# Cached attention of a four-layer decoder step: the last four value blocks of each layer are loaded into other buffers

## What is computed

```python
def memory_cross_attn(x, mem_k, mem_v, w_q, w_o):
    bsz, L, _ = x.shape
    q = (x @ w_q).reshape(bsz, L, X_HEADS, X_HEAD_DIM)
    s = jnp.einsum('blhd,bmhd->bhlm', q, mem_k.astype(q.dtype)).astype(F32) * (X_HEAD_DIM ** -0.5)
    p = jax.nn.softmax(s, axis=-1).astype(x.dtype)
    o = jnp.einsum('bhlm,bmhd->blhd', p, mem_v.astype(x.dtype)).reshape(bsz, L, D_MODEL)
    return o @ w_o
```

## Time and profile before

| what | value |
|---|---|
| median of three runs | 2028.56 us (2024.79 to 2032.39) |
| the profiled execution | 2023.7 us |
| its span, first to last instruction | 2021.8 us |
| TensorE busy (matmul) | 1951.7 us, 97% |
| VectorE, ScalarE, GpSimd busy | 62%, 46%, 50% |
| mean granted TensorE clock | 0.986 |
| HBM read and written | 292.16 MB and 29.61 MB, 159 GB/s over the span |

### The profile page before, as it was taken

One profiled execution on the slowest core, in us unless ns is written; L12 is line 12 of the kernel. 1 busy time (PEld: TensorE's weight loads), 2 busy tenths in 40 slices (PEclk: granted clock), 3 DMA queues, 4 the chain that ended last, 5 costly groups with the idle time before them and its releaser, 6 DMA issues.

```text
span 2021.8 us, 35611 instructions
## 1 busy us (share of the span) xinstructions
PE 1951.7 (97%) x13890; PEld 1760.9 (87%) x13890; DVE 1247.0 (62%) x2220; ACT 930.9 (46%) x1557; POOL 1010.1 (50%) x1249
## 2 busy tenths in 40 slices
PE   7999999998999999999999999999999999999997
PEld 5998989698888888897889999999997889999966
DVE  5988342426887778655137778777464158874452
ACT  3676522334655555342354444443242347773333
POOL 3776704036555565250346566666641347775602
PEclk8999999999999999999999999999999999999998
DMA  4444476635434444486353444444586344455860
GB/s 128 149 145 135 136 249 232 206 105 173 130 110 144 139 137 144 126 297 209 132 181 107 130 131 129 130 143 145 174 305 215 135 139 139 140 159 179 279 210 27
DMA packets 332615, 324.64 MB, mean 161 GB/s; under 512 B 19768, under 2 KB 313056, under 8 KB 332448
## 3 DMA queue, kind: packets, MB, share of 16 engines
q1 hardware_dynamic: 330944, 321.49, 49.8%
q10 hardware_dynamic: 1504, 0.87, 0.2%
HBM read 292.16 MB, written 29.61 MB: 159 GB/s over the span
## 4 chain that ended last, share of the span: by engine, by line
PE 56%; DVE 11%; ACT 4%; DMA 3%; issue 2%; POOL 1%; SPq 0%; DVEq 0%; ACTq 0%
PE ps L764 8%; PE ps L765 7%; PE ps L769 7%; PE ps L1449 4%; PE ps L1252 3%; PE ps L1458 2%; PE ps L1515 2%; PE ps L754 2%; PE ps L755 2%; PE ps L756 2%; DVE work L2534 2%; ACT wh L1704 1%; PE ps L1532 1%; PE ps L1562 1%; DMA cache_area<-cache_mem_v 1%
## 5 line engine op out<-in xcount | busy, mean ns | idle before, releaser
L1684 POOL TENSOR_TENSOR wl<-raw,wh 128x256 fp32r<-128x256 f32 x1216 | 1004.6, 862 | 983.9 <-ACT wh L1704 983.8
L1704 ACT ACTIVATE wh<-raw 128x1024 fp32r<-128x1024 f32 x304 | 311.8, 1053 | 205.2 <-PE ps L769 52.4
L764 PE MATMUL ps<-Hh,wh 128*128 128x320 f32 x1200 | 369.6, 322 | 2.6 <-DVE gate_area L2554 0.9
L765 PE MATMUL ps<-Hl,wh 128*128 128x320 f32 x1200 | 357.3, 311 | 0.0
L764 PEld LDWEIGHTS ps<-Hh,wh 128*128 128x128 f32 x1200 | 228.0, 190 | 10.4 <-DVE work L2418 1.8
L765 PEld LDWEIGHTS ps<-Hl,wh 128*128 128x128 f32 x1200 | 228.2, 190 | 2.2
L2249 DVE TENSOR_SCALAR work<-ps 128x512 f32<-128x512 f32 (+8 forms) x220 | 100.3, 474 | 171.0 <-PE ps L862 39.8
L769 PE MATMUL ps<-Hh,wl 128*128 128x320 f32 x1200 | 200.4, 309 | 0.0
L769 PEld LDWEIGHTS ps<-Hh,wl 128*128 128x128 f32 x1200 | 182.3, 188 | 0.1
L764 PE MATMUL ps<-Oh,wh 128*128 128x320 f32 x512 | 153.4, 312 | 3.7 <-DVE Ol L2995 3.7
L765 PE MATMUL ps<-Ol,wh 128*128 128x320 f32 x512 | 152.2, 310 | 0.0
(11 more groups left out here) (439 smaller groups left out, 3925.2 us busy)
## 6 DMA issues: line engine op xcount, KB each, us to landing
raw<-rg_w_in SPq DMA_DIRECT2D x128, 256.0 KB, 3.6
raw<-hg_w_in SPq DMA_DIRECT2D x128, 256.0 KB, 4.8
raw<-ssd_w_in SPq DMA_DIRECT2D x96, 256.0 KB, 4.0
work<-cache_mem_k SPq DMA_DIRECT2D x40, 512.0 KB, 6.2
raw<-rg_w_out SPq DMA_DIRECT2D x64, 256.0 KB, 3.5
raw<-x_w_k SPq DMA_DIRECT2D x64, 256.0 KB, 3.6
raw<-x_w_v SPq DMA_DIRECT2D x64, 256.0 KB, 3.8
raw<-x_w_q SPq DMA_DIRECT2D x64, 256.0 KB, 5.7
```

Of the source, the lines that this page charges most:

```text
L764: pe.matmul(ps[:, bank, 0:n], high(half, k), mh[:, k, 0:n], start=(k == 0), stop=False)
L765: pe.matmul(ps[:, bank, 0:n], high(half, k), ml[:, k, 0:n], start=False, stop=False)
L1684: ins = pool.tensor_tensor(out, src, wh[:, parted(n) % HALVES, r:r + 2].bitcast(F32), ALU.subtract)
L1704: act.activation(wh[:, nx.n % HALVES], raw[:, slot, :, half * P:(half + 1) * P], ACT.Copy).then_inc(hi_ready, 1)
```

## The change

Blocks 0 to 27 keep their buffers. Block 28 gets columns 5120 to 6143 of `work` (the prompt's memory keys), blocks 29 and 30 get the two halves of the turned keys, and block 31 gets buffer 4, in which value block 16 was. Block 28 is issued behind block 15 and ahead of block 16. Each of the three new buffers has a semaphore of its own for what has landed.

```diff
+        at_kb += [work[:, 5120:6144], work[:, 0:D], work[:, D:2 * D]]
+        KB_SLOT = [n % CACHED for n in range(28)] + [CACHED, CACHED + 1, CACHED + 2, 28 % CACHED]
 
         def cached_count(L, n):
 
-            return 16 * (L * len(range(n % CACHED, 32, CACHED)) + n // CACHED + 1)
+            return 16 * (L * KB_SLOT.count(KB_SLOT[n]) + KB_SLOT[:n + 1].count(KB_SLOT[n]))
...
-                    if n >= CACHED:
-                        sp.wait_ge(*past("at_kb_used", 32 * layer + n - CACHED + 1))
-                    sp.dma_start(at_kb[n % CACHED], src).then_inc(S(f"at_kb_in{n % CACHED}"), 16)
+                    slot = KB_SLOT[n]
+                    if slot in KB_SLOT[:n]:
+                        last = max(m for m in range(n) if KB_SLOT[m] == slot)
+                        sp.wait_ge(*past("at_kb_used", 32 * layer + last + 1))
+                    elif slot == CACHED:
+                        for h in range(2):
+                            sp.wait_ge(*past(f"at_k_out{h}", 32 * (layer + 1)))
+                    elif slot > CACHED:
+                        sp.wait_ge(*past("at_cs_full", 16 * (layer + 1)))
+                    sp.dma_start(at_kb[slot], src).then_inc(S(f"at_kb_in{slot}"), 16)
...
-                for n in range(CACHED, 32):
+                for n in [*range(CACHED, 16), 28, *range(16, 28), 29, 30, 31]:
                     cache(n)
...
                 def cached(n):
-                    pe.wait_ge(*past(f"at_kb_in{n % CACHED}", cached_count(L, n)))
-                    return at_kb[n % CACHED]
+                    pe.wait_ge(*past(f"at_kb_in{KB_SLOT[n]}", cached_count(L, n)))
+                    return at_kb[KB_SLOT[n]]
```

## The result

The changed kernel takes 2018.06 us (median of seven runs, 2010.39 to 2021.32) against 2028.56 us (seven runs, 2024.79 to 2032.39): ratio 0.9938, 95% interval 0.9923 to 0.9953. By that ratio it is 12.6 us less (9.5 to 15.6). The ratio is not the quotient of the two medians, which differ by 10.5 us only. Two later comparisons gave 0.9932 and 0.9937. The forecast was 2020.0 us in a range of 2013 to 2027. The kernel is faster by a little over 0.5%, to which I had given 0.25.

The account below looks back on a forecast made before the run. TensorE was taken to bound the kernel; 7.0 us of stall plus 1.5 us of clock, 8.5 us, took the profiled 2023.7 us to 2015.2. Adding 0.42% for the timed median gave 2020.0 us, range 2013 to 2027.

Parts of the forecast that it names:

- Stall of 29 to 31, 7.0 us: In four layers' attention, TensorE's waits for loads of value blocks 29 to 31 go away: 7.0 us in sum.
- Block 28 costs nothing: In SyncE's queue, loading block 28 early into the memory's keys costs nothing and by itself saves nothing.
- Blocks 29 and 30 go out behind the last scores: In layer 1, these loads issue at about 954.1 and 954.5 after the last score matmuls, needed 14 us after landing.
- Block 31 lands in time in first place: Issued at about 969.1 in layer 1, first in the queue, not fourth; lands 1.3 us early, without a wait.
- The tail behind block 31 moves along unchanged: From the last value block to the output projection, the same steps follow and hide nothing of the gain.
- TensorE's clock, 1.5 us: At the start of layer 3's output projection, the half-speed clock returns to full: 1.5 us, bounds 0 and 1.53.
- The sum: Over the whole kernel, 7.0 us of stall plus 1.5 us of clock give a gain of 8.5 us.
- Rival A: In the attention, block 31 stays late or part of the gain is given back: gain 3 to 5 us; chance 0.12.
- C: SyncE's queue hangs at block 28 waiting for the memory keys' stores: 2038 us or more; chance 0.02.
- D: Nothing changes, since the DMA engines can't bring the blocks earlier; chance 0.02.
- B: Half-clock stretches move elsewhere: two fewer give 2017 us, two more 2023; chances 0.12 and 0.10 for two or more.

Follow-up runs that it names:

- e7_28_in_place: The changed kernel with block 28 issued behind block 27, its old place, not behind block 15; ratio to the kernel before 0.9928.
- n1_same: The kernel before, run again with no edit; ratio to itself 0.9995, profiled span 2016.8 us.
- e4_gap: The changed kernel with TensorE made to wait for ScalarE copies ahead of value blocks 29 to 31 in all layers; ratio to the kernel before 1.0023.
- e5_values_moved: The changed kernel with half of the next layer's first memory values moved behind the value blocks in layers 0 to 2; ratio to the kernel before 0.9908.
- e3_filler: The kernel before with unused matmuls on TensorE ahead of value blocks 29 to 31 in layers 1 and 3; ratio to the kernel before 0.9985.
- n5_same: The kernel before, run again with no edit for a fourth profile; profiled span 2029.5 us.
- n3_same: The kernel before, run again with no edit for another profile; profiled span 2027.9 us.

## Why the prediction was right, and where not

- *Stall of 29 to 31, 7.0 us:* right. It went in all four layers. By the measure used above it was 7.1 us in the profile that I read and 7.7 as the mean of four.
- *Block 28 costs nothing:* right. The key phase kept its length to 0.01 us; and by e7_28_in_place it gained nothing either.
- *Blocks 29 and 30 go out behind the last scores:* right, at about 951.1 and 951.55, 20 us ahead of their use.
- *Block 31 lands in time in first place:* right in all layers of all profiles of the change (issued 966.21, used without a wait about 972.5).
- *The tail behind block 31 moves along unchanged:* right, 1.37 us before and after.
- *TensorE's clock, 1.5 us:* the mechanism right, the size too small. This is the term that was mis-sized. I took it from one execution, in which one layer of four had fallen. The four profiles have 5 falls in 16 places, 2.1 us on average and 0 to 3.7 in one execution. The changed kernel and the two later kernels without a stall (e7_28_in_place and the one with the values moved) have none in 24 places (six profiles). I also wrote that "layer 1 kept its clock": in two of the three other profiles it did not.
- *The sum:* 8.5 us forecast, 12.6 measured, 13 as the mean of three comparisons. 9.8 us of it are placed (7.7 and 2.1); some 3 us are not, as above. The median of the changed kernel came out 1.9 us from the forecast. That is nearer than the gain was, and luck has a part in it: the two medians differ by 10.5 us where the comparison gives 12.6.
- *Rival A* (31 late) fell: no wait. *C* (the queue hangs) fell: block 28 went out at once. *D* fell. *B* (the clock elsewhere): the gain is of the size that B gave for two fewer half-clock stretches, and the mean granted clock of the runs rose in every comparison. But in the profiles the stages outside are not shorter, so B is neither shown nor ruled out.
- A sign that seems to have been there and wasn't: the profiled execution, 2023.7 us, lay below all of the timed runs shown, so one could have put its losses in the attention below the typical ones. But n1_same's, 2018.7 us, was faster still and had the largest losses there, 12.5 us. What the time of an execution shows is mostly what happened elsewhere.

The Trainium skill (TensorE: Matmul & The Clock Gate, HAM oscillation) says that waits for DMA between bursts of matmuls bring the clock down; its case is one wait longer than the burst beside it. The traces agree on the direction, and e4_gap shows that it needn't be a DMA that is waited for. They also show the fall without a long wait: no single idle time printed ahead of e4_gap's value blocks was longer than 1.18 us.

## What to carry to other kernels

A buffer that is dead for the rest of a stage is worth as much as a new one: look for the last loads of a ring, whose order of release bunches them, and give only these another place. Price a stall of TensorE at its length and the slower clock that may follow, and take the second from several profiled executions, since one shows a draw and not the mean. Where TensorE must wait anyway, put work there that has to be done in any case, as e5_values_moved did.

## What was unexpected in the hardware

- Useless matmuls didn't slow the kernel and may have made it faster: e3_filler has 36 more matmul records in two layers and its loads were as late as before, and it took 3 us less (0.9985, interval 0.9969 to 1.0000).
- The same code in the same place keeps the clock in one execution and loses it in the next: layer 1 kept it with waits of 0.34, 0.72 and 0.65 us, and in n5_same with 0.53, 0.73 and 0.71 us, and lost it in n1_same behind 1.16, 0.69 and 0.64, and in n3_same behind 0.30, 0.64 and 0.63 us, the shortest of the four.
- A fall that begins early costs more than the 1.5 us I had read: in n1_same's layer 3 block 31 took 1.08 us and the way to the projection 1.62 in place of 1.37 us, and then the 16 matmuls 1.45 us more.
